# Where the one-hot rows of a product-key expert layer are multiplied by their gates: VectorE in one wide operation, or ScalarE token by token

## What is computed

```
def block(args):
    hb, eb, gb = args
    act = jax.nn.gelu(jnp.einsum("td,thkd->thk", hb, expert_u[eb]), approximate=False)
    return jnp.einsum("thk,thkd->td", act * gb, expert_v[eb])
```

## Time and profile before

| | us |
|---|---|
| median of 3 runs | 2128.77 (2128.38 to 2129.9) |
| the profiled execution, its own time | 2129.69 |
| its span, first to last instruction | 2127.8 |
| mean granted clock of TensorE, as a share of full speed | 0.969 |
| PE busy | 1960.4 (92%) |
| DVE busy | 1509.7 (71%) |
| ACT busy | 680.3 (32%) |
| POOL busy | 640.6 (30%) |

### The profile page before, as it was taken

The page is one execution under the profiler, slowest core; times in us unless marked ns, Lnnn a source line. Parts: engine busy times, 40 slices in busy tenths (PEclk is TensorE's granted clock), DMA queues, the critical chain, the costliest instruction groups (busy, mean ns, idle before and its releaser), DMA issues.

```text
span 2127.8 us, 27853 instructions
## 1 busy us (share of the span) xinstructions
PE 1960.4 (92%) x10221; PEld 1723.1 (81%) x10221; DVE 1509.7 (71%) x2752; ACT 680.3 (32%) x1247; POOL 640.6 (30%) x373
## 2 busy tenths in 40 slices
PE   2999787999978985999999999999989999999996
PEld 2789656878846884889999999999987888788885
DVE  7662257665373325678888999999769898889894
ACT  2110121001151004333444444444434444444442
POOL 1344212333212322310211352222434343334321
PEclk9999988999998997999999999999999999999998
DMA  7223203555102215225777878888999999999992
GB/s 239 90 88 99 79 0 119 171 184 178 59 1 79 79 40 178 80 77 174 262 225 226 275 256 313 297 290 289 377 377 396 394 397 397 393 396 395 396 353 74
DMA packets 251856, 467.94 MB, mean 220 GB/s; under 512 B 15545, under 2 KB 183665, under 8 KB 251761
## 3 DMA queue, kind: packets, MB, share of 16 engines
q1 hardware_dynamic: 214896, 332.54, 45.2%
q0 software_dynamic: 36864, 134.23, 16.8%
HBM read 412.19 MB, written 54.53 MB: 219 GB/s over the span
## 4 chain that ended last, share of the span: by engine, by line
PE 39%; DMA 7%; DVE 7%; issue 1%; ACT 1%; SPq 0%; POOL 0%; POOLq 0%; ACTq 0%
PE xin_ps_u L1686 23%; PE xin_out L1735 12%; DMA experts_hot<-act_scratch 7%; PE xin_out L1708 4%; DVE xin_vlo L1991 2%; DVE experts_acc L1505 1%; DVE experts_rows L1485 1%; DVE xin_wt L1988 1%; DVE in_ulo L1824 1%; DVE xin_wlo L1993 1%; ACT in_uhi L1746 0%; SPq L1659 0%; DVE in_stage L1838 0%; ACT xin_junk L1799 0%; ACT L1776 0%
## 5 line engine op out<-in xcount | busy, mean ns | idle before, releaser
L1686 PE MATMUL xin_ps_u<-con_h_hi,in_uhi 128*128 128x384 f32 x1024 | 347.6, 339 | 8.7 <-DVE in_ulo L1824 7.5
L1686 PE MATMUL xin_ps_u<-con_h_lo,in_uhi 128*128 128x384 f32 x1024 | 342.3, 334 | 0.0
L1686 PE MATMUL xin_ps_u<-con_h_hi,in_ulo 128*128 128x384 f32 x1024 | 342.3, 334 | 0.0
L1475 POOL DMA_INDIRECT experts_rows<-in_expert_rows,experts_idx x128 | 165.7, 1294 | 447.2 <-DVE experts_rows L1485 322.3
L1478 POOL DMA_INDIRECT experts_rows<-in_expert_v,experts_idx x128 | 195.7, 1529 | 318.3 <-DVE experts_acc L1505 299.9
L1735 PE MATMUL xin_out<-xin_vhi,xin_whi 128*128 128x512 f32 x768 | 238.5, 392 | 10.4 <-DVE xin_wlo L1993 10.4
L1735 PE MATMUL xin_out<-xin_vhi,xin_wlo 128*128 128x512 f32 x768 | 237.4, 390 | 0.0
L1735 PE MATMUL xin_out<-xin_vlo,xin_whi 128*128 128x512 f32 x768 | 237.4, 391 | 0.0
L1824 DVE TENSOR_TENSOR in_ulo<-con_raw,in_uhi 128x1024 fp32r<-128x1024 f32 x128 | 156.5, 1223 | 74.9 <-ACT in_uhi L1746 71.1
L1686 PEld LDWEIGHTS xin_ps_u<-con_h_hi,in_uhi 128*128 128x128 f32 x1024 | 192.4, 188 | 12.5 <-DVE in_ulo L1824 10.9
L1686 PEld LDWEIGHTS xin_ps_u<-con_h_lo,in_uhi 128*128 128x128 f32 x1024 | 192.5, 188 | 0.0
(11 more groups left out here) (328 smaller groups left out, 3901.5 us busy)
## 6 DMA issues: line engine op xcount, KB each, us to landing
con_raw<-in_expert_u SPq DMA_DIRECT2D x128, 512.0 KB
con_raw<-in_expert_v SPq DMA_DIRECT2D x128, 512.0 KB
con_raw<-in_w_in SPq DMA_DIRECT2D x38, 1024.0 KB, 5.3
act_scratch<-in_act SPq DMA_DIRECT2D x128, 192.0 KB
gate_scratch<-in_stage SPq DMA_DIRECT2D x24, 1024.0 KB
experts_hot<-act_scratch SPq DMA_DIRECT2D x128, 192.0 KB
experts_hot<-gate_scratch SPq DMA_DIRECT2D x16, 768.0 KB
xin_g<-gate_scratch SPq DMA_DIRECT2D x16, 768.0 KB
```

The lines of the kernel that those rows point to most:

```text
L1475: pool.indirect_dma_start(out=self.rows[:, r % ROWS, 0:D], out_offset=None, in_=u_table, in_offset=at).then_inc(self.u_row_in[r % ROWS], 16)
L1686: mm = pe.matmul(ps_u[s % 2][:, 0:TD], a[s % 2][:, k, :], m[:, k, P:T], start=(i == 0), stop=(i == 3 * KD - 1))
```

## The change

The multiplication by the gates leaves DVE. DVE makes the two comparisons only, and `hot_done` now stands behind the second. ACT multiplies `hot_i` in place, by 8 instructions of 128x128 in each hot step, one for each token, with the token's column of `slot[2]` as a scale of each partition. They stand at the head of ACT's hot step, ahead of `uhi` of step n+1, behind a wait for `is_row` of the same step. A new semaphore `scaled` follows the eighth, and PE waits for it, beside `hot_done`, ahead of the 8 products.

```diff
@@ PE, gates
                 m = G_STEPS * gi + q
                 pe.wait_ge(hot_done, m + 1)
+                pe.wait_ge(scaled, m + 1)
@@ ACT
+            def scale_rows(m):
+
+                act.wait_ge(is_row, m + 1)
+                for t in range(G_TOK):
+                    col = m * G_TOK + t
+                    op = act.activation(hot_i[m % 2][:, t, :], hot_i[m % 2][:, t, :], ACT.Copy,
+                                        scale=slot[2][:, col:col + 1])
+                op.then_inc(scaled, 1)
+
             def every(n):
+                if N_HOT0 <= n < N_HOT0 + N_HOT:
+                    scale_rows(n - N_HOT0)
                 if n < NEXP - 1:
 
                     cut(n + 1)
@@ DVE, gates
-                i_s, j_s, g_s = [slot[x][:, m * G_TOK:(m + 1) * G_TOK].unsqueeze(2).to_broadcast(shape) for x in range(3)]
+                i_s, j_s = [slot[x][:, m * G_TOK:(m + 1) * G_TOK].unsqueeze(2).to_broadcast(shape) for x in range(2)]
                 dve.tensor_tensor(hot_i[m % 2], keys, i_s, ALU.is_equal).then_inc(is_row, 1)
-                dve.tensor_tensor(hot_j[m % 2], keys, j_s, ALU.is_equal)
-                dve.wait_ge(is_row, m + 1)
-                dve.tensor_tensor(hot_i[m % 2], hot_i[m % 2], g_s, ALU.mult).then_inc(hot_done, 1)
+                dve.tensor_tensor(hot_j[m % 2], keys, j_s, ALU.is_equal).then_inc(hot_done, 1)
```

More of the change, by code:

```diff
@@ L1584, in experts_block @@
              "is_row"))
+        scaled = al.sem("scaled")
         vhi, vlo = [[al.sb(f"{n}{i}", [P, D], F32R) for i in range(RING)] for n in ("vhi", "vlo")]
```

## The result

| | before | changed |
|---|---|---|
| median, us | 2129.15 (4 runs, 2128.38 to 2129.9) | 2181.01 (4 runs, 2180.66 to 2181.7) |
| span of the profiled execution | 2127.8 | 2178.8 |
| DVE busy over the span | 1509.7 | 1457.5 |
| ACT busy over the span | 680.3 | 789.5 |
| mean granted clock | 0.969 | 0.973 |

The change makes the kernel slower: the ratio is 1.0244, 95% interval 1.0226 to 1.0262, about 52 us. The forecast was 2178.

A forecast was written before the change was run, and what follows sets the result against it. PE was taken to bound the hot steps before, at 5.95 us; after, a DVE-ACT ring of 6.98 us paces. 47 turns x 1.03 = 48.6 us on 2129.69 or 2128.77 gave 2178 us; 2155 to 2215 holds 8 in 10.

The forecast's parts named there:

- PE bounds the hot steps, and relief of DVE is worth nothing: Hot steps: PE sets the 48 x 5.95 us, so taking 54 us off DVE alone gains nothing.
- A scaling is 0.40 us long, 0.29 us from the next: ACT in hot steps: each of 8 scalings lasts 0.40 us, 0.29 from start to start, 2.32 us a step.
- The bounds of 0.25 and 0.40: ACT in hot steps: lower and upper bound, in us, on the distance from one scaling's start to the next.
- The 309 ns row: Trace row for a 128x128 ACT instruction from SBUF, taken as a scaling's length without its operand.
- the 90 ns of the operand: ACT scaling: extra time for an operand of each partition, 687 - 597 ns from two 128x512 groups.
- The ring of one step, 6.98 us: Hot steps, DVE and ACT: comparison, 8 scalings, `uhi`, `ulo`, gathered row in series, 6.98 us against PE's 5.95.
- the 2.32 of the sum: ACT in each hot step: 8 scalings at 0.29 us, 2.32 us.
- its 1.09: From `uhi` on ACT to the start of `ulo` on DVE: 1.05 us and 0.04 us.
- +48.6 us: Whole hot stretch: 47 turns between 48 hot steps, each 1.03 us longer, 48.6 us in all.
- Two gaps of 0.4 to 0.5 us on PE in a turn: PE in hot steps: idle before the gate group and before the next dense group, some 0.4 to 0.5 us each.
- The clock stays at 1.00: PE in the hot stretch: granted clock stays 1.00; the rival, a mean of 0.8 giving 2200 us, had 6%.
- The hidden case: Rival, hot steps: 2.32 us ahead of `uhi` is absorbed before PE wants `ulo`, time stays 2129 us; chance 8%.

The follow-up runs named there:

- the run with `uhi` first: Changed kernel with the 8 scalings on ACT behind `uhi` of the next step instead of ahead of it: 2138.71 us, ratio 1.0045 to before.
- the run with one wait: The run with `uhi` first, with the `hot_j` comparison ahead of `hot_i`'s on DVE and PE waiting for `scaled` alone: 2149.72 us, ratio 1.0096 to before.

## Why the prediction was right, point by point

- *PE bounds the hot steps, and relief of DVE is worth nothing.* Right: with the multiplication left out altogether the time is 2130.3. (The prediction read that nothing on PE waits; the trace of before has one wait of 1.2 us, for DVE, where the stretch begins, and it changes nothing.)
- *A scaling is 0.40 us long, 0.29 us from the next.* Right: 389 ns long, and from the first of the eight to `uhi` 2.36 us (1303.48 to 1305.84), 0.295 each. The bounds of 0.25 and 0.40 were wide by comparison. The 309 ns row was a little long (an instruction without the operand took 295), and the 90 ns of the operand a little short (94).
- *The ring of one step, 6.98 us.* Right in all its members and in size: 7.00 us measured (uhi from 1298.81 to 1312.81 in two turns). That it is so close is in part luck: the scalings took 0.04 us more than the 2.32 of the sum, and `uhi` up to the start of `ulo` 0.02 less than its 1.09 (1305.84 to 1306.91). Its length was tested by six and four scalings and by the constant scale, and two of its members by taking the scaling or the gathered row out of it (the others are read from the chain); each time came out within 1 us of what the ring gives, except for the 9 us of a second ring.
- *+48.6 us.* The span grew by 51.0. 47 turns at 7.00 - 5.946 = 1.054 give 49.5. The dense group behind the last products starts 50.2 us later than before (1539.30 against 1489.11), so the first turn and the passage into the loop add some 0.7 us. The other 0.8 us lies behind the hot steps, and four executions of one kernel differ by up to 1.5 us.
- *Two gaps of 0.4 to 0.5 us on PE in a turn.* Right in kind, and the first was too small. Before, the first product starts 0.17 us after the last dense matmul, and the next dense group 1.70 us after the first product. In the changed kernel these are 0.73 and 2.16 us in the straight steps and 0.86 and 2.03 in the looped ones: the products come 0.56 or 0.69 us late, the dense group 0.46 or 0.33. The first product follows the scaling's end only after 0.10 or 0.24 us, which the prediction had at nothing. (The 9.0 us of waits for `ulo` above are less than the sum of these, as they count idle time of the weight loads alone.) It did no harm, since PE had slack there. In the run with `uhi` first, where PE was in the ring, it mattered: without the 0.25 us of delay that ring of 6.21 would be 5.96 us long, about PE's own step (an estimate).
- *The clock stays at 1.00.* Right: 1.00 in 1203 to 1542, with PE pausing in every turn. By the rule of the Trainium skill named in the prediction ("TensorE: Matmul & The Clock Gate", section "A second HAM failure mode: psum-queue depth-cycling") it could have swung; with pauses of this kind the trace shows that it didn't.
- *The hidden case* fell as argued: that one step absorbs the delay says nothing when the delay returns by the next step's comparison.

What stays open: why the first product follows its release later in looped code than in straight code, and later with two waits than with one. The runs show only that it does. And the cause of the 11 us in the run with one wait is read from its chain; no run took that ring apart by itself.

## What to carry to other kernels

When work moves from a full engine to an idle one, sum the engines, but then follow the new wait in a circle: from it, down both engines' orders, until it comes back. The length of that ring in one turn, with all that stands between its members on each engine, is a bound like an engine's sum, and one position in the order can decide it. In a trace such a ring can show as two engines that each wait for the other once in every step. A chain that names one engine doesn't prove that the engine is at its own pace: compare the length of its groups with that of a run in which nothing holds it. And a nearly full engine is worth relieving only after the fullest one; here the same move lost 52 us, lost none, or gained 22, by order and by what PE had to do.

## What the runs showed of the hardware

- ACTIVATE of 128x128 from SBUF to SBUF: 295 ns, 389 ns with a scale of each partition; back to back 0.20 and 0.295 us apart, in runs of eight.
- The first of such a row, right after its wait, was followed after 0.31 us instead of 0.29 (1303.48 to 1303.79); without the operand after 0.22 instead of 0.20.
- Eight products of 128x128 in the short fp32 took 0.94 us from their start to that of the dense group behind them, in full fp32 (two parts each) 1.70: not half, 0.12 us each and 0.11 a part.
- From the end of the instruction that PE waited for to its first matmul: with two semaphores 0.24 us in looped code and 0.10 in straight code; with one 0.13 and 0.05 (in the run with one wait, and in the run with short products and the multiplication on DVE).
